# Moving the output residual from VectorE to ScalarE and GpSimd in the last stage of a diffusion step, with one VectorE instruction split in two

## The reference, cut to what matters

```
def finish(x, outs, gates, w_out, g_post, gate_mod):
    mixed = concatenate([o * silu(g) for o, g in zip(outs, gates)])     # 1024 channels
    return x + gate_mod * rmsnorm(mixed @ w_out, g_post)
```

## Time and profile before

| what | value |
|---|---|
| median of three runs | 4215.65 us (4211.58 to 4218.18) |
| the profiled execution's own time | 4218.18 us |
| its span, first to last instruction | 4216.4 us |
| busy: PE, DVE, ACT, POOL | 90%, 56%, 28%, 14% of the span |
| mean granted TensorE clock | 0.953 |
| HGRN stage of layer 1 | from about 3738 us to the end |

### The profile page before, as it was taken

How to read it: one execution, slowest core, us unless ns; L and a number is a source line. 1 busy time by engine, 2 the same in 40 slices (tenths; PEclk the granted TensorE clock), 3 DMA queues, 4 the chain that set the end, 5 groups by cost and what they waited for, 6 DMA issues and landing times. The chain is left out here.

```text
span 4216.4 us, 63526 instructions
## 1 busy us (share of the span) xinstructions
PE 3815.5 (90%) x24448; PEld 2058.2 (49%) x24448; DVE 2375.0 (56%) x4838; ACT 1201.0 (28%) x3401; POOL 576.6 (14%) x870
## 2 busy tenths in 40 slices
PE   5996999799998997699989989997999799958998
PEld 3442555445553454455544445553555445534554
DVE  3223345322667885799932333552246688868996
ACT  2401222223331121244443022232333112214444
POOL 2000000100000353101000000001000005511110
PEclk7998999899998998799999999998999999979999
DMA  7343111222213334222233021213222233332232
GB/s 230 121 143 70 55 68 53 80 74 68 83 54 115 107 120 147 75 91 100 96 121 104 38 91 48 70 41 108 72 74 74 70 121 106 107 121 102 93 112 67
DMA packets 247773, 388.91 MB, mean 92 GB/s; under 512 B 42737, under 2 KB 163441, under 8 KB 247345
## 3 DMA queue, kind: packets, MB, share of 16 engines
q1 hardware_dynamic: 207504, 262.55, 20.1%
q0 software_dynamic: 39968, 122.30, 7.9%
HBM read 264.42 MB, written 122.25 MB: 92 GB/s over the span
## 5 line engine op out<-in xcount | busy, mean ns | idle before, releaser
L1114 PE MATMUL ps<-w_sb,hT 128*128 128x512 f32 x4608 | 2197.8, 610 | 34.8 <-DMA after<-in_table 32.1
L1114 PEld LDWEIGHTS ps<-w_sb,hT 128*128 128x128 f32 x4608 | 813.1, 191 | 790.6 <-issue 750.1
L1487 PE MATMUL ps<-wo_sb,mT 128*128 128x512 f32 x1152 | 535.2, 609 | 49.5 <-ACT mT L1752 49.5
L925 POOL DMA_DIRECT2D projected<-row_t x252 | 138.7, 551 | 2600.9 <-ACT row_t L1587 1097.1
L1931 DVE RECIPROCAL e_t<-e_t 128x256 f32<-128x256 f32 (+1 forms) x180 | 430.8, 2393 | 6.2
L1487 PEld LDWEIGHTS ps<-wo_sb,mT 128*128 128x128 f32 x1152 | 210.6, 192 | 284.0 <-issue 214.5
L1929 DVE TENSOR_SCALAR e_t<-e_t 128x256 f32<-128x256 f32 (+1 forms) x180 | 63.0, 350 | 240.1 <-ACT row_t L1593 204.5
L2031 DVE TENSOR_REDUCE nei_st<-ps 128x2 f32<-128x512 f32 x72 | 49.8, 692 | 247.5 <-PE ps L1223 247.5
L2265 DVE TENSOR_TENSOR hg_q<-hg_d,hg_xT 128x256 f32<-128x256 f32 x252 | 153.8, 610 | 26.6 <-ACT hg_xT L1747 15.4
L1587 ACT ACTIVATE row_t<-ps 128x512 f32<-128x512 f32 x108 | 64.5, 598 | 347.7 <-PE ps L1114 347.7
L2064 DVE COPY nei_pT<-ps 128x512 f32<-128x512 f32 x64 | 44.3, 692 | 211.5 <-PE ps L1232 211.5
(11 more groups left out here) (241 smaller groups left out, 5308.4 us busy)
## 6 DMA issues: line engine op xcount, KB each, us to landing
projected<-row_t POOLq DMA_DIRECT2D x288, 256.0 KB, 2.3
w_sb<-in_w_in SPq DMA_DIRECT2D x14, 2048.0 KB, 10.1
wa<-in_w_ada SPq DMA_DIRECT2D x16, 1536.0 KB, 7.7
hg_raw<-projected SPq DMA_DIRECT2D x72, 256.0 KB, 4.1
out_streams<-y_t POOLq DMA_DIRECT2D x36, 512.0 KB, 4.1
hg_braw<-projected SPq DMA_DIRECT2D x108, 128.0 KB, 2.3
hg_raw<-projected SPq DMA_DIRECT2D x36, 384.0 KB, 3.9
mx_t<-mixed SPq DMA_DIRECT2D x36, 384.0 KB, 4.7
```

Of the source, the lines that this page charges most:

```text
L925: pool.dma_start(rows[tok(t), g * GRP:(g + 1) * GRP], row_t[:, p.slot]).then_inc(row_stored[p.slot], 16)
L1114: mm = nc.tensor.matmul(ps[:, p.bank, :], hT[:, k, t * P:(t + 1) * P], w_sb[:, g % 2, k, :], start=(k == 0), stop=(k == KC - 1))
L1487: mm = nc.tensor.matmul(ps[:, 6 + g, :], mT[:, t % 2, k, :], wo_sb[:, k, g * GRP:(g + 1) * GRP], start=(k == 0), stop=(k == KC - 1))
```

## The change

Three edits, all of the HGRN stage:
1. The VectorE function `residual(t)` (one `scalar_tensor_tensor` and one `tensor_tensor` over 128x1024) is removed. ScalarE gets one more instruction at the end of `scale_y(t)`: it multiplies `y_t` in place by `stat[:, b, 2:3]`. GpSimd gets two `tensor_tensor` over 128x1024, the multiplication by `gp_sb` and the addition of `xo_t`, in `add_residual(t)`, at the place where `store_y(t)` stood.
2. The wait for `wo_in` moves from VectorE to GpSimd.
3. In `level_hg`, the one update of the two tables BEYOND and AHEAD (128x256) becomes two instructions of 128x128, in levels 0 to 5.

```
-            own = Steps(pool, pool_step, l * NT * 3)
+            own = Steps(pool, pool_step, l * NT * 4)
...
-            def store_y(t):
+            def add_residual(t):
                 u, b = l * NT + t, t % 2
+                pool.wait_ge(y_scaled, u + 1)
+                nc.gpsimd.tensor_tensor(y_t[:, b], y_t[:, b], gp_sb[:, 0 if t < CT else 1], ALU.mult).then_inc(pool_step, 1)
+                pool.wait_ge(pool_step, u + 1 + 3 * NT * (l + 1))
+                pool.wait_ge(xo_in[b], 16 * (l * NP + t // 2 + 1))
+                nc.gpsimd.tensor_tensor(y_t[:, b], y_t[:, b], xo_t[:, b], ALU.add).then_inc(y_ready, 1)
                 pool.wait_ge(y_ready, u + 1)
                 pool.dma_start(streams[l + 1, tok(t), :], y_t[:, b]).then_inc(y_stored[b], 16)
...
+            pool.wait_ge(wo_in, 48 * (l + 1))
...
                 rstd(y_t[:, b], b, steps, yr_ready, y_sq[:, :])
+                act.wait_ge(yr_ready, u + 1)
+                nc.scalar.activation(y_t[:, b], y_t[:, b], ACT.Copy, scale=stat[:, b, 2:3]).then_inc(y_scaled, 1)
...
-            dve.wait_ge(wo_in, 48 * (l + 1))
...
+                def half(place, upper):
+                    y = d[:, place]
+                    return bass.AP(tensor=y.tensor, offset=y.offset + upper * s, ap=[list(y.ap[0]), [2 * s, m], [1, s]])
+
+                def whole(place, at):
+
+                    y = d[:, place]
+                    return bass.AP(tensor=y.tensor, offset=y.offset + at, ap=[list(y.ap[0]), [2 * s, m], [0, s]])
...
-                    past_end = both(BEYOND * size, size + s, 1)
-                    own.mark(nc.vector.tensor_tensor(past_end, past_end, both(size + 2 * s - 1, 1 - size - 2 * s, 0), ALU.mult))
+                    own.mark(nc.vector.tensor_tensor(half(BEYOND, 0), half(BEYOND, 0), whole(FROM_START, 2 * s - 1), ALU.mult))
+                    own.mark(nc.vector.tensor_tensor(half(AHEAD, 1), half(AHEAD, 1), whole(TO_END, 0), ALU.mult))
...
-            def residual(t):
-
-                u, b = l * NT + t, t % 2
-                dve.wait_ge(yr_ready, u + 1)
-                own.mark(nc.vector.scalar_tensor_tensor(y_t[:, b], y_t[:, b], stat[:, b, 2:3], gp_sb[:, 0 if t < CT else 1], ALU.mult, ALU.mult))
-                dve.wait_ge(xo_in[b], 16 * (l * NP + t // 2 + 1))
-                own.wait()
-                nc.vector.tensor_tensor(y_t[:, b], y_t[:, b], xo_t[:, b], ALU.add).then_inc(y_ready, 1)
...
-                if n >= 3:
-                    residual(n - 3)
...
-            residual(NT - 1)
```

More of the change, by code:

```diff
@@ L1073, in _ @@
                 if n >= 3:
-                    store_y(n - 3)
+                    add_residual(n - 3)
             pool.wait_ge(hg.s_saved, 64 * (l + 1))
@@ L2266, in level_hg @@
                 last = nc.vector.tensor_tensor(halves(k), halves(d, size + s, BEYOND * size), halves(x, size + s, size), ALU.mult)
-                def both(start, step, inner):
-                    return bass.AP(tensor=d.tensor, offset=d.offset + start, ap=[list(d.ap[0]), [step, 2], [2 * s, m], [inner, s]])
                 if lv < LEVELS - 1:
@@ L2272, in level_hg, with both @@
                     own.wait()
-                    past_end = both(BEYOND * size, size + s, 1)
-                    own.mark(nc.vector.tensor_tensor(past_end, past_end, both(size + 2 * s - 1, 1 - size - 2 * s, 0), ALU.mult))
+                    own.mark(nc.vector.tensor_tensor(half(BEYOND, 0), half(BEYOND, 0), whole(FROM_START, 2 * s - 1), ALU.mult))
+                    own.mark(nc.vector.tensor_tensor(half(AHEAD, 1), half(AHEAD, 1), whole(TO_END, 0), ALU.mult))
                 else:
                     last.then_inc(hg.qk_ready, 1)
+                def both(start, step, inner):
+                    return bass.AP(tensor=d.tensor, offset=d.offset + start, ap=[list(d.ap[0]), [step, 2], [2 * s, m], [inner, s]])
                 x_end = both(0, size + s, 1)
```

## The result

The changed kernel takes 4254.74 us (median of 4 runs, 4251.01 to 4258.54) against 4216.91 for the kernel before (4 runs, 4211.58 to 4219.58): ratio 1.0092, 95% interval 1.0074 to 1.0109. It is slower by 0.9%; 4260 was forecast, in a range of 4224 to 4298.

What follows compares the result with a forecast made beforehand. TensorE's chain was taken to bound the HGRN stage at 23.85 us a tile, VectorE close behind. Tiles 35.6, layer ends 6.8 and first tiles 1.7 made +44 us: 4260, range 4224 to 4298.

Steps and rivals of the forecast that it cites:

- The pace before: HGRN stage before the change: the chain on TensorE sets 23.85 us a tile; VectorE's own work is 23.52.
- the faster rival: VectorE's relief reaches TensorE through earlier weights; floor 22.0 us a tile without three ScalarE copies, total 4175; chance 0.05.
- The split: Table update in levels 0 to 5, two halves for one: 0.07 us a level, 0.42 a tile on VectorE.
- GpSimd: 2.36 for each product: Residual on GpSimd: each of its two products over 1024 columns takes 2.36 us, extrapolated from 256 and 512 columns.
- ScalarE: 1.06 for the multiplication, hidden: ScalarE's new multiplication over 1024 columns: 1.06 us plus 0.1 wait, inside 2.06 us of idle time.
- GpSimd's start at t0 + 10.9: GpSimd begins the residual about 10.9 us after t0, the start of the tile's first masked sum on VectorE.
- The stall of the residual: VectorE after the masked sums: GpSimd's two residual products stop its SBUF products, losing 3.7 us a tile.
- The keys' stall: GpSimd's two key products stop VectorE for 1.6 us, in levels 4 to 6 instead of level 0.
- The tile: VectorE's HGRN tile becomes 25.1 us, 1.27 over TensorE's 23.85; 28 such tiles add 35.6 us.
- The ends: Last tile of each layer, exponential to store: 6.3 us for 2.9, 6.8 us more over two layers.
- the heavier stall: Masked sums reading PSUM are stopped too, or GpSimd needs 3.0 us per product: total 4291 to 4298; chance 0.12.
- The first rival: VectorE loses under 4.03 us a tile, TensorE keeps the pace, only ends and first tiles cost: +8.5, 4224; chance 0.13.

Runs made afterwards that it cites:

- before_keys_late: Kernel before, with GpSimd's two key products waiting until TensorE has finished the previous tile's first weights; 4218.35 us (one run), tile 23.84.
- before_pe: Kernel before, with TensorE computing the first weights of the previous tile ahead of the first output projection products; 4198.19 us (one run), tile 23.43.
- no_split: Changed kernel with the single 128x256 table update kept, residual still moved to ScalarE and GpSimd; 4242.43 us, ratio 1.0051 to the kernel before.
- act_scale_only: Kernel before, with only the multiplication of y by the norm's factor moved to ScalarE; 4218.35 us (one run), tile 23.84.
- after_keys_late: Changed kernel, with GpSimd's key products waiting until TensorE has finished the previous tile's first weights; 4231.48 us, ratio 1.0015 to the kernel before.
- half_columns: Changed kernel, with GpSimd multiplying and adding only 512 of y's 1024 columns; 4228.18 us (one run), tile 23.85.
- third_product: Changed kernel, with one more GpSimd product of 128x1024 per tile ahead of the two, its result unread; 4336.29 us (one run).

## Why the prediction was right

By its steps:
- **The pace before: TensorE, 23.85 a tile, VectorE 0.32 behind.** Shown: before_keys_late takes 1.6 off VectorE for nothing, before_pe takes 0.69 of idle time off TensorE and the tile falls until VectorE stops it, at 23.43. One reading of the chain is incomplete: it leaves TensorE for four ScalarE copies a tile, not three. Between the rows shown it also passes through `y_t` at L1780 (3972.34, 0.45 us). That touches the floor of the faster rival, not the forecast.
- **The split: 0.42 a tile.** The halves measure 0.28 and 0.29, and 0.46 a tile between no_split and the changed kernel. At the start of a stage 0.85 was put down for two tiles. The first masked sum comes 0.5 later (20.6 us after the stage's start, 20.1 before and in no_split), which is the first tile's levels; the second tile shows nothing.
- **GpSimd: 2.36 for each product.** 2.37 and 2.41.
- **ScalarE: 1.06 for the multiplication, hidden.** 1.15 and hidden (act_scale_only); 0.87 of idle time is left in the changed kernel where 0.9 was put down.
- **GpSimd's start at t0 + 10.9.** 3970.85 - 3959.89 = 10.96.
- **The stall of the residual: 3.7.** 1.22 + 2.15 = 3.37. This is the term that was mis-sized: the second product was stretched by 0.04, not by the 0.3 taken over from the shorter instructions of the earlier trace rows, so GpSimd was done at t0 + 15.8 and not 16.0. That is 0.2 of the 0.36. The rest is in how the sum counts VectorE: q and k together advance its queue by 4.17 us (3971.86 to 3976.03) where they take 0.79 without a stall, and the sum took off only one of the two instructions and left out the 0.3 us that VectorE ends behind GpSimd.
- **The keys' stall: 1.6, now in levels 4 to 6.** 1.69.
- **The tile: 25.1.** 24.90, so 28 x 1.05 = 29 us in place of 35.6 (29.9 by the masked products' starts). This term is as large as the miss of 6 us between the forecast (+44) and the measured 37.8. That the totals come so close is partly luck: the sum is about the stages, and these grew by 34.3 in the two traces, 36.4 without the one long step of layer 0; the rest of the 37.8 lies outside them or in the scatter of whole runs.
- **The ends: 6.3 for 2.9, 6.8 in all.** 6.3 (4240.86 to 4247.18), and 3.3 more than before in each layer.
- **The masked sums are not stopped.** Shown in after_keys_late; this, and GpSimd's 2.37 us where that rival had 3.0, rules out the heavier stall.
- **The wait for `wo_in`: nothing.** It was not tried alone. The stage's first transpose still waits for that load in the changed kernel.
- **The range.** The 4298 and the 4175 are reckoned from the profiled execution's 4218.18, the 4260, 4224 and 4291 from the median 4215.65. It moves them by 2.5 us and decides nothing.

The first rival (under 4.03 us of stall only ends and first tiles cost) was not the case here, but it is right about the threshold: after_keys_late is this case, with 3.7 us of stall and +7.6 us. The faster rival had its mechanism half right: VectorE's relief pays, but only once TensorE's own idle time is gone, and not by this move.

## What to carry to other kernels

Work taken off VectorE is not gone when it goes to GpSimd: here 2.52 us became 3.37 us of stall, and took the stall of the next GpSimd products along into VectorE's way. Before moving work off an engine ask whether the chain waits for it at all; when it doesn't, the best that the move can do is to cost nothing. If GpSimd has to multiply in SBUF, put it beside VectorE instructions that read PSUM, and look for idle time on the engine that the chain does name: one reordering on TensorE's side gave 21 us in these stages.

## What the runs showed of the hardware that was not expected

- A GpSimd instruction with one input (128x1024, 2.77 us) is slower here than one with two (2.37), and yet holds VectorE's two-input products only until 1.3 to 1.4 us after its own start. Two-input ones held the products that met them to their own end and 0.2 to 0.3 us more (3973.50, 3975.99 and 3978.21 against 3973.22, 3975.71 and 3978.05), but for one that gets through between two of them.
- Two-input GpSimd products also stopped a VectorE copy of 128x2, 2.15 us for 0.17 to 0.24.
- GpSimd loses too: in half_columns the two key products and two VectorE products take turns, and the key products take 0.90 us each, where they take 0.74 and 0.73 in the changed kernel.
- When VectorE sets the pace, TensorE's clock can fall: in third_product, with waits of 1.86 us in 18 of 28 tiles, the granted clock is 0.86 to 0.93 in most stretches of the stage; in the changed kernel, with waits of 1.02 us, it is 1.00 in all from 3850 to 4200. Eight of the 18 tiles with that wait kept the full clock, so the wait alone does not decide it.
